# Attention stage: the low weight parts of three projection tiles made on POOL instead of VectorE

## The reference, cut to what matters

```
for l in range(2):
    h    = rms(x) * norm1_g
    proj = h @ w_in                      # 1024 x 7680, the "projection"
    o_a  = sliding_window_attention(...) # softmax over bands of 128 keys, with sinks
    o_b  = rwkv7_time_mix(...)           # a recurrence, here solved in chunks of 128 tokens
    o_c  = retention(...)
    x    = x + (g0*o_a + g1*o_b + g2*o_c) @ w_out
    x    = x + (silu(h2 @ w_gate) * (h2 @ w_up)) @ w_down
second_block(x)                          # 16 experts, 1 x 1024 x 2048 x 3 weights each
```

## Time and profile before

| | us |
|---|---|
| median of 3 runs (2176.33 to 2178.39) | 2178.12 |
| the profiled execution, its own time | 2175.79 |
| its span, first to last instruction | 2173.9 |
| busy: PE | 1803.5 (83%) |
| busy: DVE | 941.3 (43%) |
| busy: ACT | 556.0 (26%) |
| busy: POOL | 30.2 (1%) |

### The profile page before, as it was taken

The page is one execution under the profiler, slowest core; times in us unless marked ns, Lnnn a source line. Parts: engine busy times, 40 slices in busy tenths (PEclk is TensorE's granted clock), DMA queues, the critical chain, the costliest instruction groups (busy, mean ns, idle before and its releaser), DMA issues.

```text
span 2173.9 us, 31021 instructions
## 1 busy us (share of the span) xinstructions
PE 1803.5 (83%) x13580; PEld 1235.2 (57%) x13580; DVE 941.3 (43%) x1331; ACT 556.0 (26%) x636; POOL 30.2 (1%) x23
## 2 busy tenths in 40 slices
PE   8999999999999999999999987665656566666665
PEld 7998788888999878888878742121111111111111
DVE  7787578666778658765587520000000000000000
ACT  4555023444356212443463020000000000000001
POOL 0000000000000010000000000000000000000000
PEclk9999999999999999999999999887888888887888
DMA  8443645656543364556644689999999999999997
GB/s 288 160 155 131 243 154 173 194 153 215 193 157 128 145 262 142 168 181 168 207 152 156 272 343 427 427 427 429 429 428 428 428 428 429 429 429 428 427 428 320
DMA packets 189606, 613.29 MB, mean 282 GB/s; under 512 B 8344, under 2 KB 105145, under 8 KB 164281
## 3 DMA queue, kind: packets, MB, share of 16 engines
q1 hardware_dynamic: 186928, 602.04, 71.1%
q10 hardware_dynamic: 2568, 9.63, 1.3%
HBM read 610.60 MB, written 1.05 MB: 281 GB/s over the span
## 4 chain that ended last, share of the span: by engine, by line
PE 50%; DMA 37%; DVE 9%; ACT 3%; issue 1%; ACTq 0%; SPq 0%; DVEq 0%; PEldq 0%
DMA work<-in_w_down 13%; DMA work<-in_w_up 12%; DMA work<-in_w_gate 12%; PE PS L1998 10%; PE PS L1999 5%; PE PS L1902 3%; PE PS L1980 3%; PE PS L1973 3%; PE PS L1975 3%; PE PS L1102 3%; PE PS L1866 2%; DVE ring_low L2740 1%; PE PS L794 1%; PE PS L1118 1%; PE PS L2012 1%
## 5 line engine op out<-in xcount | busy, mean ns | idle before, releaser
L1102 PE MATMUL PS<-work,proj 128*32 128x512 f32 x1024 | 155.4, 741 | 98.4 <-DMA work<-in_w_up 59.2
L1704 DVE TENSOR_TENSOR proj<-proj,PS 128x512 f32<-128x512 f32 x16 | 11.0, 687 | 495.4 <-PE PS L1102 495.4
L1998 PE MATMUL PS<-x_both,high_f 128*128 128x512 f32 x608 | 210.9, 396 | 0.0
L1999 PE MATMUL PS<-x_both,ring_low 128*128 128x256 f32 x704 | 195.7, 278 | 0.0
L1102 PE MATMUL PS<-ring,proj 128*32 128x512 f32 x768 | 118.5, 748 | 84.3 <-DMA ring<-in_w_up 46.1
L2723 DVE TENSOR_TENSOR ring_low<-ring,high_f 128x4096 fp32r<-128x4096 f32 (+1 forms) x38 | 146.8, 3863 | 26.6 <-ACT high_f L2459 26.5
L1102 PEld LDWEIGHTS PS<-work,proj 128*32 128x32 f32 x1024 | 31.2, 123 | 216.5 <-DMA work<-in_w_up 96.9
L2459 ACT ACTIVATE high_f<-ring 128x4096 fp32r<-128x4096 f32 (+1 forms) x38 | 121.1, 3187 | 114.3 <-PE PS L1999 96.3
L1395 ACT ACTIVATE proj<-PS 128x512 f32<-128x512 f32 x16 | 9.6, 597 | 515.5 <-PE PS L1102 515.5
L1999 PEld LDWEIGHTS PS<-x_both,ring_low 128*128 128x128 f32 x704 | 132.3, 188 | 0.0
L1708 DVE TENSOR_TENSOR proj<-PS,xT 128x512 f32<-128x512 f32 x32 | 20.7, 686 | 251.5 <-PE PS L1118 234.9
(11 more groups left out here) (556 smaller groups left out, 3535.6 us busy)
## 6 DMA issues: line engine op xcount, KB each, us to landing
ring<-in_w_in SPq DMA_DIRECT2D x73, 1024.0 KB, 7.2
work<-in_w_gate SPq DMA_DIRECT2D x32, 2048.0 KB, 35.6
work<-in_w_up SPq DMA_DIRECT2D x32, 2048.0 KB, 36.1
work<-in_w_down SPq DMA_DIRECT2D x28, 2048.0 KB, 35.9
ring<-in_w_up SPq DMA_DIRECT2D x25, 2048.0 KB, 35.7
ring<-in_w_gate SPq DMA_DIRECT2D x23, 2048.0 KB, 35.8
ring<-in_w_down SPq DMA_DIRECT2D x22, 2048.0 KB, 36.7
ring<-in_w_ada SPq DMA_DIRECT2D x24, 1024.0 KB, 8.5
```

The source lines that it names most:

```text
L1102: mm = nt.matmul(PS[32 * j:32 * j + 32, 2 + n // 4, :], x(k), w[:, F_E * kk + 512 * j:F_E * kk + 512 * (j + 1)], start=(k == 0), stop=(k = ...
L1998: nt.matmul(PS[:, at + b, :], h[:, c:c + P], both[:, k, :], start=(k == 0), stop=False, skip_group_check=True)
L1999: mm = nt.matmul(PS[:, at + b, 0:T], w[:, c:c + P], both[:, k, 0:T], start=False, stop=(k == kn - 1), skip_group_check=True)
```

## The change

The low parts of blocks 25, 27 and 29 are taken out of DVE's program and put into POOL's, between the memsets at the start of the layer and the memset L1841. POOL waits for ACT's high part of the block and then subtracts, two TENSOR_TENSORs of 128x1024 per block; they count on a new semaphore `low_pool`, for which PE waits ahead of the low part's matmuls of these blocks. `low_count` leaves the three blocks out.

```diff
+POOLED = [25, 27, 29]
 def low_count(l, n, half=1):
-    return part_count(l, n, half) + (half if (l, n) == (0, 2) else l > 0 or n > 2)
+    pooled = len(POOLED) * l + sum(p < 2 * n + half for p in POOLED)
+    return part_count(l, n, half) + (half if (l, n) == (0, 2) else l > 0 or n > 2) - pooled
...
                 pool.memset(Q1, 0.0).then_inc(q1_zero, 1)
+                for q in POOLED:
+                    n = q // 2
+                    pool.wait_ge(high_ready, part_count(l, n, q % 2))
+                    for b in range(2):
+                        c = tile_columns(q, b)
+                        cut = lambda a: a[:, n % RING, :].rearrange("p (k c) -> p k c", c=512)[:, :, c:c + P]
+                        ins = pool.tensor_tensor(cut(ring_low), cut(ring), tile_high(q, b).rearrange("p (k c) -> p k c", c=P).bitcast(F32),
+                                                 ALU.subtract)
+                    ins.then_inc(low_pool, 1)
                 pool.wait_ge(oa_out, 3)
...
-                if b == 0:
+                if b == 0 and q in POOLED:
+                    pe.wait_ge(low_pool, len(POOLED) * l + POOLED.index(q) + 1)
+                elif b == 0:
                     pe.wait_ge(low_dve, low_count(l, n, q % 2))
...
                     tile_lows(l, 24 + 2 * rnd)
                     solve(SOLVED[2 * rnd + 1], SOLVED[2 * rnd + 2])
-                    tile_lows(l, 25 + 2 * rnd)
                 solved_blocks()
```

More of the change, by code:

```diff
@@ L431, in build @@
         high_ready, low_dve, vec_order = sem("high_ready"), sem("low_dve"), sem("vec_order")
-        half_taken = sem("half_taken")
+        half_taken, low_pool = sem("half_taken"), sem("low_pool")
         group_sums, group_taken = sem("group_sums"), sem("group_taken")
```

## The result

The changed kernel takes 2185.36 us (median of 8 runs, 2184.29 to 2188.01) against 2177.43 us before (8 runs): ratio 1.0039, 95% interval 1.0028 to 1.0050. It is slower by 0.39%, some 8 us; the prediction's forecast was 2186.9 us. The profiled execution has a span of 2183.8 us; it was 2173.9.

The account below looks back on a forecast made before the run. DVE's queue of solve steps, low parts and softmax was taken to set the pace, with PE nearly full. Losses of 2.2 + 2.2 us per layer, 8.8 in all, on 2178.12 gave 2186.9 us; range 2171.5 to 2190.5.

Parts of the forecast that it names:

- The turns: DVE solve steps beside POOL: a step with two SBUF inputs stands for POOL's whole instruction, some 2.25 us.
- The signs: Profile times: second-round scale and mask near 177.4 us, PE's block 26 high part 186.3, solved-block transposes 218.5.
- Block 25: Second round: two solve steps held by POOL, so scale and mask start 2.2 us later per layer.
- Block 27: Third round: DVE has only instructions with one SBUF input beside POOL, so nothing is lost.
- Block 29: Last solve steps: two holds add 4.5 us, the removed pair gives back 2.28; transposes 2.2 us later.
- The uncontended gain: Second and last rounds, with POOL's work free: 2.85 us per layer, 5.7 us in all.
- The second rival: Solve steps at 202 to 207 us: DVE reads freely, POOL fits between; 5.2 to 5.7 us faster, chance 0.25.
- reaches the end in full: DVE's path in the layers sets the pace, so a gain or loss there should carry fully to the kernel's end.
- The forecast of 8.8 us: Loss in both layers together: 2.2 us in the second round plus 2.2 us behind the last, per layer.
- The third rival: Both rounds' POOL work: 3.39 us per instruction by itself, blocking DVE too; 10.4 us lost per layer, chance 0.05.
- The 0.45 us for each of eight instructions: Added to the forecast for each POOL instruction that DVE meets, giving the range's upper end of 2190.5 us.

Follow-up runs that it names:

- e4: Changed kernel with POOL writing zeros (memsets) instead of subtracting for blocks 25, 27 and 29: 2169.44 us, ratio 0.9971 to the kernel before.
- e3: Changed kernel with only block 27 on POOL, 25 and 29 back on DVE: 2176.37 us, ratio 1.0003 to the kernel before.
- e9: Changed kernel with each POOL subtraction cut into four of 256 elements: 2181.07 us against 2177.44 us for the kernel before.
- e11: Changed kernel with 7 extra matmuls on PE behind block 29: 2185.47 us against 2176.42 us for the kernel before.
- e1: Changed kernel with only block 25 on POOL, 27 and 29 back on DVE: 2181.35 us against 2176.16 us for the kernel before.
- e8: Changed kernel with 12 extra matmuls on PE behind block 29: 2186.54 us against 2177.44 us for the kernel before.
- e5: Changed kernel with the solve steps' unknowns copied to PSUM, POOL's subtractions kept: 2170.86 us, ratio 0.9975 to the kernel before.

## Why the prediction was right

*The turns, the step on which all hangs.* It was read off one row, where POOL stood behind DVE, and taken as a mirror for DVE behind POOL. The mirror holds: 2.35 to 2.48 us for eight steps in the two layers. The Trainium skill (SBUF — State Buffer, section "Who interferes with whom") has it as a rule that a DVE instruction with two SBUF inputs contends with a GpSimd instruction that reads SBUF, and not with one that only writes it. The traces agree: 3.39 us for POOL's instruction behind DVE, 2.35 us for DVE's step behind POOL, and steps of 0.29 us beside the memsets of e4.

*The signs.* With the 0.94 us taken off, the scale and mask of the second round starts at 177.01 (predicted near 177.4), the high part of block 26 on PE at 186.01 (near 186.3) and the transposes of the solved blocks at 218.65 (near 218.5). The last is closer than it should be, as 0.9 us of it is a clock dip.

*Block 25.* Two steps, +4.1 us, less 2.28: 1.87 us, predicted 2.2. The term was sized with 2.25 us for each hold on top of a step's own length; measured is 2.06 (2.35 - 0.29), as the step's own time lies inside the hold.

*Block 27.* Nothing, as predicted; e3 shows it alone.

*Block 29.* The steps of 2.48 and 2.37 us instead of 0.27 each, 4.3 us, less 2.28 are 2.0; L2915 is 0.2 us shorter, which no run here explains; 1.8 at PE, predicted 2.2.

*The uncontended gain.* 2.85 us per layer in the working, 2.89 with the memsets and 2.87 to 2.89 with the unknowns in PSUM. The second rival had the right price and the wrong condition.

*What the prediction did not have.* It left TensorE's clock out, which was 1.00 in the stretch that it looked at the earlier trace rows. The dips add 3.0 us in the layers, and 1.6 us come back in the first expert, so "reaches the end in full" is not quite so. The forecast of 8.8 us is met by 7.4 of holds and some 1.4 of clock (8.7 at the first expert, 8.96 at the end of the profile, 7.9 between the medians). The mechanism was right. That the sum is so near is in part luck: the holds were put 1.4 us too high, and the clock, put at nothing, is about as much the other way.

*The third rival* rested on POOL's 3.39 us as its own pace; its subtractions take 2.36 to 2.47. The 0.45 us for each of eight instructions at the upper end of the range was a margin that no row gave.

## What to carry to other kernels

Before work is moved from DVE to POOL, list what DVE runs beside it and count its inputs in SBUF: here a DVE TENSOR_TENSOR with two of them stood until POOL's reading instruction had ended, and the short steps of a dependent chain were the worst company, 0.3 us becoming 2.4. One input in PSUM was enough to make the same move pay 5 to 6 us. In a profile, look for instructions of an unchanged shape that have become as long as a neighbour's; the waits don't show them.

## What the runs showed that I had not expected

The granted clock of TensorE fell to half in or behind each of PE's long waits for the solved blocks (2.63 to 3.54 us): in the changed kernel and its repetition, with block 29 alone and with POOL cut in four, eight of eight. Most of these dips lasted 3 to 4 us; both with block 29 alone and one in e9 lasted about twice that. In the other runs no wait of PE there is longer than 1.1 us, and no dip comes. But dips also came behind shorter waits: in the changed kernel, its repetition and e11 near 187 us, behind waits of about 1.3 and 1.0 us, while the same two waits brought none in e1 and e8; in e11 near 712 us; in the kernel before near 1271 us; in e5 near 282 us, even with PE busy 3.95 of the 4.0 us from 276. These wander from kernel to kernel. Each dip is worth 0.8 to 2.2 us, as much as the terms that were to be told apart. What decides about these smaller ones stays open.

In e9 a TENSOR_SCALAR of 128x4 with a single input, beside POOL, also took long, 0.68 us instead of 0.17 (DVE's timeline, second round; 0.67 in layer 1):

```profile
177.04 0.48 DVE L3030 TENSOR_TENSOR small<-small,par 128x4 f32<-128x4 f32 x1
177.56 0.68 DVE L3031 TENSOR_SCALAR small<-small 128x4 f32<-128x4 f32 x1
```

The scale and mask (one input in PSUM) and the maximum (a single input, in SBUF) stayed at 1.22 to 1.23 us beside POOL throughout. Whether one input spares an instruction thus depends on its kind; no run here sorts the kinds out.
